# The first input projection: SP issues the next pair's first weight load ahead of the stores of the last two result tiles

## The reference

```python
mod = jax.nn.silu(c) @ ada_w[layer] + ada_b[layer]
sh_m, sc_m, g_m, sh_f, sc_f, g_f = jnp.split(mod[:, None, :], 6, axis=-1)
h = rms_norm(x, norm_mix_w[layer]) * (1.0 + sc_m) + sh_m
proj = h @ w_in_ab[j]                 # 1024 x 4368
oa, ... = rwkv7_mixer(proj[..., :A_COLS], ...)
ob, ... = mamba2_mixer(proj[..., A_COLS:], ...)
```

## Time and profile before

| | us |
|---|---|
| median of 3 runs | 3695.66 |
| lowest and highest | 3694.4, 3708.12 |
| profiled execution, its own time | 3701.06 |
| its span | 3699.3 |
| stretch of the 17 groups and the rest tile | about 40 to 562 |

### The profile page before, as it was taken

The page is one execution under the profiler, slowest core; times in us unless marked ns, Lnnn a source line. Parts: engine busy times, 40 slices in busy tenths (PEclk is TensorE's granted clock), DMA queues, the critical chain, the costliest instruction groups (busy, mean ns, idle before and its releaser), DMA issues. The chain is left out here.

```text
span 3699.3 us, 69879 instructions
## 1 busy us (share of the span) xinstructions
PE 3471.2 (94%) x29337; PEld 3250.4 (88%) x29337; DVE 2204.6 (60%) x3207; ACT 1286.4 (35%) x2226; POOL 1795.8 (49%) x1388
## 2 busy tenths in 40 slices
PE   7999996999999999999999899989979999999998
PEld 6887875777669899999999899987769899999998
DVE  7656555774885665555544845547766755555446
ACT  5333334663641243333200344435541433332000
POOL 3766653120003377777532378850033677776331
PEclk8999998999999999999999999999989999999999
DMA  6655541101432022222332133333352122223322
GB/s 220 182 180 177 164 159 44 33 23 43 107 100 97 29 65 72 72 72 72 123 94 75 55 123 123 129 125 88 104 150 69 48 72 72 72 72 114 97 88 75
DMA packets 399217, 358.51 MB, mean 97 GB/s; under 512 B 20531, under 2 KB 364113, under 8 KB 393790
## 3 DMA queue, kind: packets, MB, share of 16 engines
q1 hardware_dynamic: 398256, 353.49, 30.0%
q0 software_dynamic: 128, 0.02, 0.2%
q10 hardware_dynamic: 526, 0.60, 0.1%
HBM read 259.40 MB, written 94.68 MB: 96 GB/s over the span
## 5 line engine op out<-in xcount | busy, mean ns | idle before, releaser
L1102 PE MATMUL ffn_acc<-ffn_BH,ffn_WH 128*128 128x384 f32 x1232 | 417.9, 339 | 22.7 <-DVE ffn_BL L1321 12.5
L1102 PE MATMUL ffn_acc<-ffn_BL,ffn_WH 128*128 128x384 f32 x1232 | 416.0, 338 | 0.0
L1102 PE MATMUL ffn_acc<-ffn_BH,ffn_WL 128*128 128x384 f32 x1232 | 415.4, 337 | 0.0
L1037 POOL TENSOR_TENSOR ffn_WL<-raw,ffn_WH 128x512 fp32r<-128x512 f32 x176 | 283.1, 1610 | 259.4 <-ACT ffn_WH L1191 259.4
L2121 PE MATMUL ffn_acc<-ffn_BH,ffn_WH 128*128 128x384 f32 x1056 | 353.7, 335 | 7.1 <-DVE ffn_BL L2185 4.3
L2121 PE MATMUL ffn_acc<-ffn_BL,ffn_WH 128*128 128x384 f32 x1056 | 353.4, 335 | 0.0
L1037 POOL TENSOR_TENSOR ffn_WL<-ffn_S,ffn_WH 128x512 fp32r<-128x512 f32 x176 | 274.6, 1570 | 33.8 <-ACT ffn_WH L1191 33.8
L1102 PEld LDWEIGHTS ffn_acc<-ffn_BH,ffn_WH 128*128 128x128 f32 x1232 | 233.4, 189 | 29.9 <-POOL ffn_WL L1037 14.2
L2194 DVE SCALAR_TENSOR_TENSOR xT<-ffn_acc,mod,xT 128x768 f32<-128x768 f32 x96 | 97.6, 1017 | 254.3 <-PE ffn_acc L2121 254.3
L1102 PE MATMUL ffn_acc<-ffn_hH,ffn_WH 128*128 128x394 f32 x704 | 240.5, 342 | 4.2 <-DVE ffn_hL L1353 3.3
L1102 PE MATMUL ffn_acc<-ffn_hH,ffn_WL 128*128 128x394 f32 x704 | 241.2, 343 | 0.0
(11 more groups left out here) (735 smaller groups left out, 9485.3 us busy)
## 6 DMA issues: line engine op xcount, KB each, us to landing
spare<-in_ada_w SPq DMA_DIRECT2D x42, 1024.0 KB, 7.3
pT<-xT SPq DMA_DIRECT2D x50, 576.0 KB, 3.7
hidden<-ffn_up SPq DMA_DIRECT2D x44, 576.0 KB, 2.8
raw<-in_w_gate SPq DMA_DIRECT2D x44, 512.0 KB, 3.8
raw<-in_w_up SPq DMA_DIRECT2D x44, 512.0 KB, 3.8
raw<-in_w_down SPq DMA_DIRECT2D x80, 256.0 KB, 2.8
raw<-in_w_in_ab SPq DMA_DIRECT2D x34, 512.0 KB, 7.0
raw<-in_w_in_c SPq DMA_DIRECT2D x32, 512.0 KB, 4.1
```

The costliest lines, as they stand in the source:

```text
L1037: self.nc.gpsimd.tensor_tensor(self.WL[:, slot], src, self.WH[:, slot].bitcast(F32), ALU.subtract).then_inc(lo, 1)
L1102: ins = self.nc.tensor.matmul(self.acc[:, bank, 0:n], w[:, slot, k, :], x(low, k), start=start and k == 0 and w is self.WH and low == 0, s ...
```

## The change

Within one pass j of SP's loop, the next group's `load1` moves ahead of both stores, and the third block load of the pass comes to stand between the stores. Nothing else changes: the same transfers, the same sizes, the same waits with each of them.

```diff
                 later.load(sp, ada, 3 * j - 1)
-                store(2 * j - 2)
                 later.load(sp, ada, 3 * j)
-                store(2 * j - 1)
                 if j + 1 < N:
                     m.load1(sp, j + 1, columns(j + 1, 0))
                 else:
                     sp.wait_ge(m.s3_set, N)
                     sp.dma_start(g.raw[:, 0, :, 0:rest], src[:, :, NAB * P:IN_AB]).then_inc(rest_in, 16)
+                store(2 * j - 2)
                 later.load(sp, ada, 3 * j + 1)
+                store(2 * j - 1)
                 if j + 1 < N:
                     m.load2(sp, j + 1, columns(j + 1, 1))
```

## The result

The changed kernel takes 3673.43 us, the median of five runs (3666.57 to 3676.89), against 3700.84 us for the kernel before in the same comparison (3694.4 to 3708.12). The ratio is 0.9925 with a 95% interval of 0.9906 to 0.9944: faster by 27.8 us, between 21 and 35. The profiled executions differ by 30.4 us in their spans, 3699.3 and 3668.9.

A forecast was written before the change was run, and what follows sets the result against it. PE was taken to bound the kernel, busy 94% of the span, leaving only its idle time to win: 29.3 + 1.64 + 1.4 = 32.4 us. Less 1.6 for POOL's chain, 3695.66 - 30.8 = 3664.9 us, range 3660 to 3671.

The forecast's parts named there:

- The bound: PE's idle time in the projection's groups: at most 32.4 us to gain, as 29.3 + 1.64 + 1.4.
- four transposes stand for a step: In four of 42 step slots PE's work was estimated about 0.4 us shorter each, some 1.6 us in all.
- The forecast: Whole kernel: 30.8 us off the median 3695.66, giving 3664.9 us; chance 0.62.
- POOL's chain: POOL's work from A12 to S4's low part ends 0.2 us late in eight late groups, costing 1.6 us.
- the two drops of the clock: PE's clock at 250 to 260 and 356 to 386: they go with the waits, about 3.5 us together.
- The load: SP's load1, moved past both stores: issued 13.8 us into the group, landing at 17.9; A11 waits go.
- All seven waits go: PE's waits for DVE at L1904: DVE ready at 30.4, needed at 34.2, so seven waits of 1.4 us go.
- rival B: Only PE's waits for A11 go and DVE's stay: gain 19.6 us, time 3676; chance 0.10.
- The second store: SP's store behind the third block load: lands by 25.7 us against a limit of 28.4, costing PE nothing.
- Rival C: Second store lands late, ACT's copy holds PE in seven groups: gain eaten, or slower at 3710 us; chance 0.03.
- Rival A: POOL's chain or load2 takes over, 2.1 us in eight groups: gain 15.6, time 3680; chance 0.18, whole or half.

The follow-up runs named there:

- small_late: Changed kernel with POOL's four small loads moved from group 3 to behind its last group; 3662.83 us, ratio 0.9898.
- bias_first: Kernel before, with ACT's bias of the first tile moved ahead of its wait for the next group's A11; 3673.46 us, ratio 0.9922.
- bias_last: Changed kernel with ACT's bias of the first tile moved behind the copy and the cast of A12; 3700.02 us, ratio 0.999.
- block_last: Changed kernel with the second store back ahead of the third block load; 3666.57 us, ratio 0.9912.
- late_store: Changed kernel with each pass's second store moved behind load2 and the next block load; 3711.72 us, ratio 1.0019.

## Why the prediction was right, point by point

*The bound.* 32.4 us from a group without idle time. With the small loads out of the way the stretch shrank by 34.1 us and PE has no pause left in groups 2 to 16; the bound was 1.7 us short. Of that, 1.3 us are one term: where four transposes stand for a step I took 0.4 us off the group, an estimate with no row behind it. The runs show 0.7: group 13 of small_late goes from 405.37 to 431.38, 26.0 us and not 26.73, and there are four such groups.

*The forecast.* 30.8 us; measured 29.7 in the stretch and 27.8 by the ratio. 3664.9 was forecast from a median of 3695.66 over three runs; with five it is 3700.84, which accounts for 5.2 of the 8.5 us between forecast and median. That 30.8 and 29.7 lie so close is in part luck: the 1.6 us set aside for POOL's chain were not needed, the bound was 1.7 short, and a pause that I had not seen cost 4.4; 30.8 + 1.6 + 1.7 - 4.4 = 29.7. Groups 2 to 15 took 375.6 us (373 to 376 said), PE's waits 4.6 us (under 4 said, missed by the pause in group 3), ACT's wait for raw weights 3.7 us (under 40 said), and the two drops of the clock went.

*The load.* Issued "at 13.8", landing "at 17.9", and alone. It went out at 9.0 and took 6.4 us: 15.4. Two terms were off, by 4.8 us one way and 2.3 the other, and cancelled in part. I kept S3's end where it was, though it hung on the loop; and the load was not alone, since the block for the step before far(A22), whose own place I had costed at nothing, goes out at 415.5, 1.3 us ahead of it.

*DVE.* "All seven waits go", right. But the two kinds of wait were summed as if either could go alone, and rival B was built on that. bias_first and bias_last show one loop: cutting it on ACT alone wins 26.6 us, and making the bias late again loses 23.8. The prediction named both places rightly, and took for a chain with two harms what goes round in a circle.

*The second store.* Landing "at most" 25.7, limit 28.4: measured 425.41 + 7.0 = 432.4, at 24.6. The hidden wait is shown by block_last, the limit by late_store. Rival C's formula held (5.9 against 5.69 us); only the number of groups in it was seven for five.

*A12 and POOL's chain.* I took 1.6 us for a chain that might end 0.2 us late in eight groups. It ended early: from S1's start at 408.23 to S3's end 8.5 us instead of 11.7, since the convolution was no longer beside it (bias_last, where it is beside it again: 12.4). Rival A did not come.

*What I missed* is the 3.9 us in group 3. The 15.6 us of the earlier trace rows were in hand, with POOL's small transfers named as the cause; I used them for a rival about stores, and did not ask which transfer would stand there in the new order.

The clock behaved as the sum assumed, with no drop from 81.5 to 532. The Trainium skill (TensorE: Matmul & The Clock Gate, "What's actually happening") says that activity releases the low clock; the trace agrees, with 1.00 at 240 to 260 and 356 to 386.

## What to carry to other kernels

Where two waits of the bottleneck engine recur with the same period, follow each around the whole loop before adding them up: a late transfer, a late instruction queued behind it, and a late store ahead of the next transfer were one fault with two cheap cures, and either alone brought about nine tenths of the gain or more. When a transfer is moved earlier, look up what else is on the DMA engines at its new time, small transfers of many packets above all. An engine's new wait of 38.8 us cost nothing, and the limit at which it would have cost could be worked out beforehand from one group without idle time.

## What the runs showed of the hardware

Four loads with 0.02 MB and 128 packets in all held up a 512 KB load from another queue, with a block and a store ahead of it, by some 8 us (17.0 in the changed kernel, 8.6 in small_late). DVE's convolution and POOL's sums slow each other: in group 13 of the kernel before, POOL's L1044 took 2.19 us beside L1941, and at 147.60 in the changed kernel, with DVE idle, 1.27; the three L1941 together took 7.31 us beside POOL and 4.40 us in group 13 of the changed kernel, where POOL was idle from 427.59 to 433.50:

```profile
428.27 4.40 DVE L1941 SCALAR_TENSOR_TENSOR xT<-xT,colB 128x1176 f32<-128x1176 f32 x3
```

That mutual slowing is the link of the loop between the late convolution and the late sums.
